# Order of the first requests in an expert stage: gate and up weights, further gate and up weights, further down weights

## What is computed

```
e_p, e_idx = lax.top_k(jax.nn.softmax(e_logits, axis=-1), TOPK_IN_GROUP)
...
def expert_block(args):
    xb, e = args
    return (jax.nn.silu(xb @ w_gate[e]) * (xb @ w_up[e])) @ w_down[e]
...
out = jnp.zeros((N, D), jnp.float32).at[buf_t].add(ys.astype(jnp.float32) * buf_w[:, None])
```

## Time and profile before

| | us |
|---|---|
| median of 3 runs | 1762.95 |
| the 3 runs | 1757.38, 1762.95, 1766.21 |
| the profiled execution, its own time | 1760.23 |
| its span | 1758.9 |
| TensorE busy | 1651.4 (94%) |
| VectorE busy | 921.0 (52%) |
| ScalarE busy | 694.0 (39%) |
| GpSimd busy | 350.5 (20%) |

### The profile page before, as it was taken

The page is one execution under the profiler, slowest core; times in us unless marked ns, Lnnn a source line. Parts: engine busy times, 40 slices in busy tenths (PEclk is TensorE's granted clock), DMA queues, the critical chain, the costliest instruction groups (busy, mean ns, idle before and its releaser), DMA issues.

```text
span 1758.9 us, 25433 instructions
## 1 busy us (share of the span) xinstructions
PE 1651.4 (94%) x9824; PEld 1198.7 (68%) x9824; DVE 921.0 (52%) x1861; ACT 694.0 (39%) x1518; POOL 350.5 (20%) x356
## 2 busy tenths in 40 slices
PE   6999889999999999999997799999999988999992
PEld 5887569878888888877876466668888753333330
DVE  4752664455777665673526866643436652232224
ACT  4432752353333334454323677764424421121111
POOL 0000644102222210000000455530010122333320
PEclk9999999999999999999998799999999999999997
DMA  6321000322444444323200000015223359999964
GB/s 271 120 96 48 1 2 3 144 96 93 186 174 175 186 180 156 132 96 144 96 0 25 1 8 8 8 43 228 96 97 143 144 195 385 396 388 374 391 234 161
DMA packets 40230, 251.76 MB, mean 143 GB/s; under 512 B 17904, under 2 KB 18032, under 8 KB 23600
## 3 DMA queue, kind: packets, MB, share of 16 engines
q1 hardware_dynamic: 23120, 223.49, 32.4%
q10 hardware_dynamic: 3168, 15.07, 2.3%
q0 software_dynamic: 13824, 11.58, 2.1%
HBM read 293.99 MB, written 18.87 MB: 178 GB/s over the span
## 4 chain that ended last, share of the span: by engine, by line
PE 85%; DVE 6%; DMA 4%; ACT 2%; issue 1%; SPq 0%; POOL 0%; ACTq 0%; POOLq 0%; DVEq 0%
PE banks L2236 17%; PE banks L2238 16%; PE banks L2237 16%; PE banks L2716 9%; PE banks L2164 6%; PE banks L2732 4%; PE banks L2297 3%; PE banks L2321 3%; DMA plain<-in_moe_gu,arena 2%; PE banks L2423 1%; PE banks L2178 1%; PE banks L2589 1%; DVE units L1222 1%; PE banks L2632 1%; PE banks L2557 0%
## 5 line engine op out<-in xcount | busy, mean ns | idle before, releaser
L641 ACT ACTIVATE units<-arena 128x512 fp32r<-128x512 f32 (+2 forms) x416 | 250.8, 626 | 470.3 <-PE banks L2238 466.2
L1222 DVE TENSOR_TENSOR units<-arena,units 128x512 fp32r<-128x512 f32 x370 | 252.3, 705 | 276.2 <-ACT units L641 275.9
L2236 PE MATMUL banks<-hx,units 128*128 128x512 f32 x800 | 314.6, 393 | 4.3 <-DVE arena L1675 1.7
L2238 PE MATMUL banks<-hx,units 128*128 128x512 f32 x800 | 312.1, 390 | 0.0
L2237 PE MATMUL banks<-hx,units 128*128 128x512 f32 x800 | 311.9, 390 | 0.0
L2236 PEld LDWEIGHTS banks<-hx,units 128*128 128x128 f32 x800 | 150.6, 188 | 36.1 <-issue 5.3
L2238 PEld LDWEIGHTS banks<-hx,units 128*128 128x128 f32 x800 | 150.6, 188 | 31.9
L2237 PEld LDWEIGHTS banks<-hx,units 128*128 128x128 f32 x800 | 150.7, 188 | 30.4
L641 ACT ACTIVATE arena<-banks 128x512 f32<-128x512 f32 (+3 forms) x194 | 106.5, 564 | 140.8 <-PE banks L2164 63.2
L2236 PE MATMUL banks<-units 128*128 128x512 f32 x380 | 148.9, 392 | 3.9 <-DVE units L1222 3.9
L2238 PE MATMUL banks<-units 128*128 128x512 f32 x380 | 147.9, 389 | 0.0
(11 more groups left out here) (420 smaller groups left out, 2526.3 us busy)
## 6 DMA issues: line engine op xcount, KB each, us to landing
arena<-in_moe_gu SPq DMA_DIRECT2D x32, 2048.0 KB, 10.0
arena<-in_w_in SPq DMA_DIRECT2D x17, 2048.0 KB, 9.0
arena<-in_moe_dn SPq DMA_DIRECT2D x32, 1024.0 KB, 9.0
arena<-in_ada SPq DMA_DIRECT2D x12, 2048.0 KB, 11.1
arena<-in_w_gu SPq DMA_DIRECT2D x11, 2048.0 KB, 8.4
arena<-in_w_out SPq DMA_DIRECT2D x4, 2048.0 KB, 8.6
arena<-in_w_down SPq DMA_DIRECT2D x4, 2048.0 KB, 9.9
arena<-in_cmp_w SPq DMA_DIRECT2D x2, 2048.0 KB, 8.3
```

What stands on the lines that cost most here:

```text
L641: return func(dst, src, ACT.Copy, scale=scale)
L1222: tt(lo, src, hi.bitcast(F32), SUB).then_inc(*up("gemm_dve", "lo", c.part, u))
L2236: pe.matmul(bs[i], sh[:, q], mh, start=c.first and k == 0, stop=False)
L2238: return pe.matmul(bs[i], sl[:, q], mh, start=False, stop=c.last and k == c.kn - 1)
```

## The change

```diff
@@ pool_program @@
     halves(0)
     gather(m.gx[1], 1, "gx1", 1)
-    downs(0)
     g.wait_ge(*at("moe_pe", "xT", 0, 1))
     gather(m.gx[0], 2, "gx0", 2)
@@ loop over the pairs @@
         if i + 1 < NPAIR:
             g.wait_ge(*at("moe_pe", "gud", i))
             halves(i + 1)
+            if i == 0:
+                downs(0)
         if i + 3 < NPAIR:
@@ sp_program @@
+        if name == "moe5":
+            for half in range(2):
+                sp.wait_ge(*at(f"dyn_gu{half}", 1))
         load(name)
```

## The result

The changed kernel is slower. Its median is 1772.34 us over 8 runs (1761.20 to 1774.27), that of the kernel before 1760.73 us over 8 runs; the measured ratio, which is not the quotient of the two medians, is 1.0048 with a 95% interval of 1.0032 to 1.0065, so about 0.5% slower. The forecast was 1756.3 us. The profiled execution, 1761.20 us, is the fastest of the eight, 11 us under the median. So its trace shows the mechanism, but not its usual size; two more traces of the same kernel follow among the experiments (again, again2).

What follows compares the result with a forecast made beforehand. TensorE, busy 1651.4 of 1758.9 us, was taken as the bound. Removing 4.22 us of wait and 2.49 us of slow clock (-6.7 us) from the median of 1762.95 gave 1756.3 us, range 1752.5 to 1761.5.

Steps and rivals of the forecast that it cites:

- What bounds the kernel: Whole kernel: TensorE is busy 1651.4 of 1758.9 us, so only its idle or slow time for transfers can be won.
- the wait goes: Ahead of gud 1: halves(1) lands before gu 1 ends, so TensorE's idle time goes, gain 4.22 us.
- the slow clock goes: At gud 1: its 16 matmuls run at full clock, 3.60 us instead of 6.09, gain 2.49 us.
- moe5 is requested later: SyncE's load for gu 2: issued at about 1458.1 instead of 1447.00, takes 10 us, cost nothing; at most 2.0 us.
- The next further gather: halves(2), for gud 2: issued 6.7 us earlier, its second request takes 11.0 us, no wait; at 13.0 a 1.9 us wait.
- The two later waits: Ahead of gud 4 (0.65 us) and gud 8 (1.44 us): assumed to stay as they are.
- the bandwidth rival: Whole stage: bandwidth sets the end, each gather waits and the gain is given back, 1762.95 us; chance 0.08.
- downs(0) moves: GpSimd's further down weights, now behind halves(1): some 32 us of cover, scatter and token gather 2.6 us later at most.
- The next gather takes a part: halves(2) takes 13.0 us, gud 2 waits 1.9 us: time 1758.2, or 1760.6 with a slow clock; chance 0.17.
- The rival for slower: halves(1) lands at 1465.8 as before, moe5 is issued only then, gu 2 waits 3.0 us: 1768.5 us; chance 0.04.
- The chances: Forecast 0.60; for faster by over 0.5%, half of "more is won" and a quarter of the forecast: 0.06 + 0.14 = 0.20.

Runs made afterwards that it cites:

- again: The changed kernel, unchanged, run again for a second trace: median 1775.07 us, ratio 1.0069 to the kernel before.
- again2: The changed kernel, unchanged, a single execution for a third trace, on another chip: 1775.66 us.
- wait_all: The changed kernel with every second load of a pair (moe5, moe7 to moe31) waiting for the further gate and up weights requested last: 1764.25 us, ratio 1.0017.
- downs_only: The kernel before with only the move of downs(0) behind halves(1), without SyncE's new wait: 1760.44 us, ratio 0.9996.
- wait_only: The kernel before with only SyncE's wait for halves(1) ahead of moe5, downs(0) staying early: 1762.56 us, ratio 1.0011.
- after_split: The changed kernel with each gate and up load of SyncE in two requests of 8 KB rows instead of one of 16 KB rows: 1751.82 us, ratio 0.9942.
- after_split4: The changed kernel with each gate and up load in four requests of 4 KB rows: 1749.12 us, ratio 0.9937.
- before_split4: The kernel before, without the change, with each gate and up load in four requests of 4 KB rows: 1750.79 us, ratio 0.9942.
- after_split4_b: The same kernel as after_split4, measured a second time: 1751.12 us, ratio 0.9944.

## Why the prediction was wrong

*What bounds the kernel; the wait goes; the slow clock goes.* Right, to the number: the second request of halves(1) landed in 6.0 us, the value taken, gud 1 did not wait and ran in 3.60 us, and from gu 1 to gu 2 TensorE took 16.85 us instead of 23.71, 6.9 us less.

*moe5 is requested later.* Right: issued at 1456.5, it landed in 8.5 us (10 was taken), and no trace of the study shows a wait for it.

*The next further gather.* This step failed. "The nearest is 11.0 ... I take that: no wait" stood on bounds of 4.1 and 13.0 us. It took 14.1 us in the profiled execution and 13.2 and 13.4 in the two other traces, above the upper bound. That bound was also misread: 13.0 is not the slowest of such requests in the rows, halves(1) itself had taken 13.7. And I did not ask what makes up the 11 us. The packets give it: 2.8 us until GpSimd's first packet and 18 turns of 0.61 us. Nothing of GpSimd's own stood ahead of this gather, the scatter of pair 0 had landed at 1464.9. The cost is 2.0 to 3.0 us, and 1.75 of slow matmuls.

*"The two later waits ... I leave as they are."* This failed too, and is the larger part: gud 4 went from 0.65 us to 4.20, 13.12 and 12.20 in three traces. The slack of 27 us in 220 that I worked out against the bandwidth rival is real (in wait_all no dense load comes late). But I read it as room for the dense loads alone. As long as it isn't used up to clear the backlog, each gather meets a full queue. In the kernel before, the wait at gud 1 itself, as I read it, let the queue run dry: between 1462 and 1478.6 SyncE requested nothing, and 162 GB/s moved from 1476 to 1480. In the changed kernel the requests that left at 1478.6 leave at 1470.1. What was removed as a loss had also been what cleared the way for halves(2).

*downs(0) moves, cost nothing.* Right for itself (downs_only), wrong in company: with SyncE's wait it is the difference between two long executions in twelve (wait_only) and fourteen in fifteen (the changed kernel, again, again2).

*The rivals.* "The next gather takes a part" named the place and a fuller queue as the reason, with 1.9 us as its price; it was 3.0 and slow matmuls, and it went on to the next gathers. What I held against it, that most rows of such a request are skipped, is wrong: a skipped row costs a turn like any other. That the profiled execution, 1761.20 us, lies next to the 1760.6 of this rival is luck, since gud 4 took its part too and 1.6 us were won ahead of gu 1. The rival for slower (halves(1) not quicker, moe5 late) didn't happen. The bandwidth rival's outcome, gain given back, is what wait_only shows, by the turns of packets and not by a lack of bytes per us: after_split moves the same bytes and is 20 us faster.

*The chances.* A quarter of 0.60 is 0.15, not 0.14; it changes nothing.

**The long execution.** In it the gather for gud 4 needs 22.5 to 23.4 us, and 18 turns of 0.61 us are 11. GpSimd's own queue has the rest. Its requests landed in the order in which they were issued, and this is the last scatter that it issued ahead of halves(4) (issue to landing, us; in the kernel before, the changed kernel, again, again2, issued at 1500.75, 1497.12, 1497.63, 1502.24):

```profile
y_rows<-arena POOLq DMA_INDIRECT x1, 6.2
...
y_rows<-arena POOLq DMA_INDIRECT x1, 21.5
...
y_rows<-arena POOLq DMA_INDIRECT x1, 24.1
...
y_rows<-arena POOLq DMA_INDIRECT x1, 23.3
```

Before, it had landed at 1507.0, ahead of halves(4). In the three executions with the change it landed 12 to 14 us after the second request of halves(4) had been issued. So this gather stands in line behind downs(1) and a scatter, and their rows pay their turns too. From 1522 to 1530 us of the trace of again the queues read:

```profile
q1 hardware_dynamic: 228, 3.33, 97.5%
q0 software_dynamic: 116, 0.05, 2.3%
```

GpSimd's packets are half of SyncE's, so only a part of the engines still has rows of GpSimd's to serve. The landings tell how many. A request raises its semaphore 16 times (`by=16`), as I read it once by each engine, and the trace keeps the moments. For the second request of downs(1) they are, in the kernel before, all within 1504.1 to 1506.7 us; in the changed kernel thirteen up to 1504.7 and three from 1514.9 to 1515.6; in again eight up to 1505.6 and eight from 1517.1 to 1519.1; in again2 eight up to 1510.0 and eight from 1520.3 on. With no late engine the gather for gud 4 took 11.0 us, with three 14.5, with eight 23.4 and 22.5.

**Open.** It stays open why three engines are late in one execution and eight in another, and so why one execution of the changed kernel in fifteen was spared. As I read it, it is a race: SyncE's next two loads leave at 1500.59 in the changed kernel and at 1504.23 before, and an engine that has not done with downs(1) when their rows of 16 KB arrive must take turns with them from there on. No run tests that.

The fastest versions are after_split4 (1749.1 and 1751.1 us in two series) and before_split4 (1750.8): 0.6% below the kernel before, by an edit in `load` that leaves the order of the requests as it was and adds no wait.

## What to carry to other kernels

Before a large transfer is held back for a small late one, ask what the small one pays for: if two queues take turns by packet, many small or even empty packets wait for one long packet each, the small one also waits for those of its own queue that pay in the same way ahead of it, and cutting the long rows helps at every place at once, where holding back helps at one. And a stall in a stage whose DMA engines are full is also the time in which they catch up: when it is removed, look at the next transfers of the same kind with the queue as it will then be, and not as the trace shows it.

## What the hardware showed unexpectedly

- Rows of an indirect DMA that are skipped by their bounds check still cost a turn each: 170 packets with 0.00 MB against 170 of SyncE's, mostly of 16 KB, in 6 us, and 223 against 223, mostly of 8 KB, in 4 us.
- Rows of 4 KB cost no time against rows of 16 KB in the dense loads: in after_split4 and after_split4_b TensorE never waited for them, in a stage that moves 386 GB/s in one trace and 393 in the other.
- The same program had executions of 1761 and of 1768 to 1779 us, and the difference between the two traced on either side was mostly one gather that landed after 14.5 or after 23.4 us, with three or eight of 16 engines late.
